# A ring of eleven places, unrolled programs and halved last loads in a mixer and MoE block

## The reference

```python
logits = xt @ w_router + b_router
top_val, top_idx = lax.top_k(logits, 4)          # of 32 experts
gate = softmax(top_val)
# for each expert e, on the tokens that chose it:
hdn = xb @ w_mlp1[e] + b_mlp1[e]                 # 1024 -> 2048
glu = minimum(hdn[:, :1024], 7); lin = clip(hdn[:, 1024:], -7, 7)
act = glu * sigmoid(1.702 * glu) * (lin + 1)
y = act @ w_mlp2[e] + b_mlp2[e]                  # 1024 -> 1024
# out = rmsnorm(x + sum_k gate_k * y_k) * norm_final_w
```

## Time and profile before

| | |
|---|---|
| median of 3 runs | 1125.36 us (1125.34 to 1125.79) |
| the profiled execution, its own time | 1125.41 us |
| its span | 1123.6 us |
| granted PE clock over the span | 0.998 |
| PE busy | 1085.1 us, 97% |
| DVE, ACT busy | 367.8 and 245.6 us |
| moved by DMA | 439.15 MB, mean 391 GB/s |
| the chain that ended last | PE 79%, DMA 14%, DVE 6% |

### The profile page before, as it was taken

One profiled execution on the slowest core, in us unless ns is written; L12 is line 12 of the kernel. 1 busy time (PEld: TensorE's weight loads), 2 busy tenths in 40 slices (PEclk: granted clock), 3 DMA queues, 4 the chain that ended last, 5 costly groups with the idle time before them and its releaser, 6 DMA issues.

```text
span 1123.6 us, 14458 instructions
## 1 busy us (share of the span) xinstructions
PE 1085.1 (97%) x5409; PEld 487.5 (43%) x5410; DVE 367.8 (33%) x813; ACT 245.6 (22%) x345; POOL 3.6 (0%) x12
## 2 busy tenths in 40 slices
PE   9999999999999999999999999999999999999996
PEld 8888888533333333333333333333333333333332
DVE  5977787422222222222222222222222222212223
ACT  4845674311111111111111111111111111111112
POOL 0000000000000000000000000000000000000000
PEclk9999999999999999999999999999999999999999
DMA  9655469999999999999999999999999999999996
GB/s 336 223 157 165 155 204 417 428 420 416 428 427 436 430 430 429 432 428 433 435 432 395 429 433 435 433 432 432 430 429 430 433 435 432 432 432 430 426 423 253
DMA packets 37877, 439.15 MB, mean 391 GB/s; under 512 B 5244, under 2 KB 5432, under 8 KB 21880
## 3 DMA queue, kind: packets, MB, share of 16 engines
q1 hardware_dynamic: 37488, 437.78, 93.3%
q10 hardware_dynamic: 360, 0.95, 0.3%
HBM read 437.67 MB, written 1.05 MB: 390 GB/s over the span
## 4 chain that ended last, share of the span: by engine, by line
PE 79%; DMA 14%; DVE 6%; issue 0%; ACT 0%; SPq 0%; DVEq 0%; PEldq 0%; ACTq 0%
PE bank L1154 33%; PE bank L1181 18%; DMA ring<-in_w_mlp_dram 11%; PE bank L798 9%; DMA late_slots<-in_w_mlp_dram 4%; PE bank L1083 3%; PE bank L1165 2%; PE bank L792 2%; PE bank L963 2%; PE bank L1011 2%; DVE xn L1670 2%; DVE xn L1667 2%; DVE xn L1674 2%; PE bank L1059 1%; PE bank L1067 1%; PE bank L1133 1%
## 5 line engine op out<-in xcount | busy, mean ns | idle before, releaser
L1154 PE MATMUL bank<-ring,xn 128*64 128x512 f32 x1232 | 276.3, 595 | 6.3 <-DMA ring<-in_w_mlp_dram 6.3
L1154 PE MATMUL bank<-late_slots,xn 128*64 128x512 f32 x880 | 197.5, 596 | 4.9 <-DMA late_slots<-in_w_mlp_dram 4.9
L1154 PEld LDWEIGHTS bank<-ring,xn 128*64 128x64 f32 x1232 | 84.4, 136 | 163.8 <-issue 150.3
L1181 PE MATMUL bank<-ring,smo 128*64 128x512 f32 x624 | 138.3, 595 | 0.0
L705 ACT ACTIVATE xn<-bank 128x512 f32<-128x512 f32 x33 | 19.7, 598 | 481.5 <-PE bank L1154 481.5
L1154 PEld LDWEIGHTS bank<-late_slots,xn 128*64 128x64 f32 x880 | 60.2, 136 | 117.9 <-issue 106.3
L1683 DVE SCALAR_TENSOR_TENSOR moe_y_lo<-bank,st,moe_y_hi 128x512 fp32r<-128x512 f32 x33 | 24.8, 750 | 235.5 <-ACT moe_y_hi L712 235.5
L1667 DVE TENSOR_SCALAR xn<-bank 128x512 f32<-128x512 f32 x33 | 22.8, 691 | 220.9 <-PE bank L1154 220.9
L1181 PE MATMUL bank<-late_slots,smo 128*64 128x512 f32 x416 | 92.1, 595 | 0.0
L1181 PEld LDWEIGHTS bank<-ring,smo 128*64 128x64 f32 x624 | 42.9, 137 | 81.1 <-issue 81.1
L712 ACT ACTIVATE moe_y_hi<-bank,st 128x512 fp32r<-128x512 f32 x33 | 22.7, 687 | 233.7 <-PE bank L1181 233.7
(11 more groups left out here) (270 smaller groups left out, 890.9 us busy)
## 6 DMA issues: line engine op xcount, KB each, us to landing
ring<-in_w_mlp_dram SPq DMA_DIRECT2D x43, 4096.0 KB, 30.4
late_slots<-in_w_mlp_dram SPq DMA_DIRECT2D x29, 4096.0 KB, 28.0
ring<-in_w_mlp_dram SPq DMA_DIRECT2D x28, 2048.0 KB, 13.4
late_slots<-in_w_mlp_dram SPq DMA_DIRECT2D x15, 2048.0 KB, 15.6
ring<-in_w_in_dram SPq DMA_DIRECT2D x22, 1024.0 KB, 5.4
late_slots<-in_w_mlp_dram SPq DMA_DIRECT2D x8, 1024.0 KB, 38.5
ring<-in_w_branch_dram SPq DMA_DIRECT2D x4, 1024.0 KB, 5.0
ring<-in_w_out_dram SPq DMA_DIRECT2D x4, 1024.0 KB, 7.1
```

The lines of the kernel that those rows point to most:

```text
L1154: last = mm(B[4 + u][g * C:(g + 1) * C, :], xgT[:, k % 4, k // 4, :], by_group(held[k // 2][0][:, k % 2, u * FF:(u + 1) * FF], g), start=F ...
L1181: last = mm(B[7][g * C:(g + 1) * C, :], actT[:, j, h * C:(h + 1) * C], held[4 + h][0][:, j // 2, (j % 2) * D + g * N:(j % 2) * D + (g + 1) ...
```

## The change

The place used once becomes the eleventh place of the ring: a chunk m sits in place m % 11 throughout. The places lie in two rows of memory, five in `late`, six in `ring`, and a quad of 4 MB must not cross the end of a row; so a pair whose first place is 3 or 9 is loaded as two DMAs of 2 MB. To give the eleventh place room beside `late`, `smo` is moved behind `sgm`. The order of the first 11 loads changes, their gates keep their counts. The loops of five experts are gone: SP's and PE's programs are written out for all experts (the run-time loop around each item stays). In the last loads of W1 (i = 3) and W2 (i = 5) the second MB is split into two halves of 0.5 MB, each with its own semaphore. The b2 scatter is issued before expert 16, not before expert 6. At the end, DVE takes the mean of the second tile between the two output halves of the first.

```diff
-PLACES = 10
-ROUND = PLACES // 2
-QUADS = range(ROUND + 1, E - 2)
+FIRST_QUADS = 6
+PLACES = 11
+QUADS = [m for m in range(CHUNKS * FIRST_QUADS, CHUNKS * (E - 2), 2) if m % PLACES not in (3, PLACES - 2)]
...
-        late_pair = [late[:, 2 * i:2 * i + 2, :] for i in range(4)]
-        places = [late_pair[1], pair[0], pair[1], pair[4], pair[5], pair[2], pair[3], late_pair[2], late_pair[3], late_pair[0]]
-        once = nc.alloc_sbuf_tensor_at("place_used_once", [P, 2, SLOT], F32, offset=sga_at)
+        late_pair = [late[:, 2 * i:2 * i + 2, :] for i in range(5)]
+        places = late_pair[1:5] + pair + late_pair[0:1]
+        quads = {n: late[:, at:at + 4, :] for n, at in ((PLACES - 1, 0), (0, 2), (1, 4), (2, 6))}
+        quads.update({4 + n: ring[:, 2 * n:2 * n + 4, :] for n in range(5)})
...
+        half_landed = {3: landed[4], 5: landed[5]}
...
                 if pieces == 2:
-                    for half, done in enumerate((place_landed[place], piece_landed[i])):
-                        sp.dma_start(places[place][:, half, :], src[:, half * SLOT:(half + 1) * SLOT]).then_inc(done, 16)
+                    at = [0, SLOT, 2 * SLOT] if i % 2 == 0 else [0, SLOT, SLOT + FF, 2 * SLOT]
+                    for a, b, done in zip(at, at[1:], (place_landed[place], piece_landed[i], half_landed.get(i))):
+                        sp.dma_start(places[place].rearrange("p a n -> p (a n)")[:, a:b], src[:, a:b]).then_inc(done, 16)
...
+            for e in range(E - 1):
+                after = sp.value_load(first_item[0:1, e + 1:e + 2], min_val=1, max_val=ITEMS - 1)
+                for i in range(CHUNKS):
+                    m = CHUNKS * e + i + PLACES
+                    if m >= CHUNKS * E:
+                        continue
+                    if m not in QUADS and m - 1 not in QUADS:
+                        wait_freed(after, i)
+                        load(m // CHUNKS, m % CHUNKS, m % PLACES, 2 if m >= CHUNKS * (E - 1) + 2 else 1)
+                    elif m - 1 in QUADS:
+                        wait_freed(after, i)
+                        load_quad(m // CHUNKS, m % CHUNKS // 2, (m - 1) % PLACES)
...
                     for u in range(2):
+                        if u and k == KB - 1 and 3 in in_halves:
+                            pe.wait_ge(*in_halves[3])
...
+                        if j == 3 and 4 + h in in_halves:
+                            pe.wait_ge(*in_halves[4 + h])
...
-            with pe.Fori(1, (E - 2) // ROUND) as r:
-                experts(r, lambda c: chunks_in_round(c, r))
+            for e in range(1, E - 1):
+                if e == E // 2:
+                    pe.wait_ge(opened, 2 * TT)
+                    scatter_b2()
+                first = after
+                after = pe.value_load(first_item[0:1, e + 1:e + 2], min_val=1, max_val=ITEMS - 1)
+                with pe.Fori(first, after) as i:
+                    item(i, chunks(e))
...
-            final_scale(0)
+            final_rstd(0)
+            final_half(0, 0)
             final_mean(1)
-            final_scale(1)
+            final_half(0, 1)
+            final_rstd(1)
+            final_half(1, 0)
+            final_half(1, 1)
```

More of the change, by code:

```diff
@@ L115, in landings @@
     for m in range(CHUNKS * E):
[L116 to L121, removed]
+        place = m % PLACES
+        if m - 1 in QUADS:
             table.append(table[-1])
@@ L158, in build @@
         xhi_at = late_at
-        late = nc.alloc_sbuf_tensor_at("late_slots", [P, 2 * HALF, SLOT], F32, offset=late_at)
+        late = nc.alloc_sbuf_tensor_at("late_slots", [P, 2 * HALF + 2, SLOT], F32, offset=late_at)
         xhi_room = sb("xhi_room", [P, KB, S])
@@ L406, in load_quad @@
                 sp.dma_start(quads[place].rearrange("p a n -> p (a n)"), src).then_inc(place_landed[place], 16)
+            def load_quad(e, g, place):
+                if g < 2:
+                    src = w_mlp1[0, e, g * N:(g + 1) * N, :].rearrange("(p s) n -> p (s n)", s=ROWS)
+                else:
+                    src = w_mlp2[0, e].rearrange("(p s) n -> p (s n)", s=2 * ROWS)
+                sp.dma_start(quads[place].rearrange("p a n -> p (a n)"), src).then_inc(place_landed[place], 16)
@@ L418, in _ @@
             sp.wait_ge(slots_used, Q_OUT + 2)
-            load(1, 0, 5)
-            load(1, 2, 7)
+            first_load(1)
+            first_load(6)
             sp.wait_ge(slots_used, Q_MOE)
-            load(1, 1, 6)
-            load(1, 3, 8)
-            load(1, 4, 9)
+            first_load(2)
+            first_load(7)
+            first_load(10)
             sp.wait_ge(firsts, 1)
[L427 to L442, removed]
+            for e in range(E - 1):
[5 more added lines that the diff above has]
+                    if m not in QUADS and m - 1 not in QUADS:
@@ L451, in _ @@
[L451 to L456, removed]
+                        load_quad(m // CHUNKS, m % CHUNKS // 2, (m - 1) % PLACES)
             after = sp.value_load(first_item[0:1, E - 1:E], min_val=1, max_val=ITEMS - 1)
-            wait_freed(after, 2)
+            wait_freed(after, 3)
@@ L1101, in chunks, with item @@
             def chunks(e):
[L1103 to L1122, removed]
+                at = [(m, *landing[m]) for m in range(CHUNKS * e, CHUNKS * (e + 1))]
+                return [(places[m % PLACES], place_landed[place], 16 * count) for m, place, count in at]
             def by_group(columns, g):
                 return columns.rearrange("p (q g s) -> p g q s", g=2, s=ROWS)[:, g]
-            def item(i, held, in_pieces={}):
+            def item(i, held, in_pieces={}, in_halves={}):
                 pe.wait_ge(row_ready, i + 1)
@@ L1184, in item @@
                     last.then_inc(slots_used, 2)
+            items = pe.value_load(first_item[0:1, E:E + 1], min_val=1, max_val=ITEMS - 1)
             with pe.Fori(0, after_first) as i:
[L1187 to L1202, removed]
-            with pe.Fori(1, (E - 2) // ROUND) as r:
-                experts(r, lambda c: chunks_in_round(c, r))
-            with pe.Fori(last_first, items) as i:
-                item(i, chunks(E - 1), {c: (piece_landed[c], 16 * (SLOTS[:Q_MOE].count(c - 2) + 1)) for c in piece_landed})
+                item(i, chunks(0))
+            after = after_first
+            for e in range(1, E - 1):
[6 more added lines that the diff above has]
+                    item(i, chunks(e))
+            with pe.Fori(after, items) as i:
+                item(i, chunks(E - 1), {c: (piece_landed[c], 16 * (SLOTS[:Q_MOE].count(c - 2) + 1)) for c in piece_landed},
+                     {3: (half_landed[3], 16 * (SLOTS[:Q_MOE].count(4) + 1)), 5: (half_landed[5], 16 * (SLOTS[:Q_MOE].count(5) + 1))})
             pe.wait_ge(gT_ready, items + 1)
@@ L1696, in final_scale, with final_half @@
                 dve.wait_ge(rstd, 2 * TT + t + 1)
[L1697 to L1700, removed]
+            def final_half(t, n):
+                cut = slice(n * N, (n + 1) * N)
+                v.scalar_tensor_tensor(out=xn[:, t, cut], in0=B[2 * t + n][:, :], scalar=st[:, 6 + t:7 + t],
+                                       in1=wfin[:, cut], op0=ALU.mult, op1=ALU.mult).then_inc(normed, 1)
             dve.wait_ge(s_small2, 16)
```

37 lines of the change are left out of this document (15 added, 22 removed).

## The result

| | before | changed | ratio, 95% interval |
|---|---|---|---|
| median of 7 runs | 1125.36 us | 1129.14 us | 1.0037 [1.0027, 1.0047] |
| profiled execution, its span | 1125.41, 1123.6 us | 1130.57, 1128.8 us | |

The change makes the kernel 3.8 us slower. 1127.2 was forecast, with 1122.6 to 1130.0 as the range: the time lies in the range, and the sign of the sum was right, but its size was half of what came. The profiled execution is one of the slower of the seven, 1.4 us above their median, so what its trace shows is somewhat larger than in the median run.

What follows compares the result with a forecast made beforehand. PE bounds roughly the first 25 experts, the weight stream the last ones. The terms sum to +1.8 us on the time before (median 1125.36), giving 1127.2 us, range 1122.6 to 1130.0.

Steps and rivals of the forecast that it cites:

- PE and SP written out: Weight stream after 503 us: some 22 more instruction blocks, three more visits to the worst DMA engine, +3.0 us.
- first dip, ring of eleven: Stream short of work at 240 to 260 us; eleven places let loads issue some 4 us sooner, -1.2 us.
- second dip: Stream dry at 590 to 610 us, the expert with two items; filling it gains 0, since late engines lose nothing there.
- 14 pairs: Weight loads: 14 of 72 quads become 28 loads of 2 MB at a slightly lower rate, +1.3 us.
- order of first loads: Expert 0's chunks 1 and 2 load later but still before PE reads them, 0 us.
- halves: PE's last W1 wait: four of eight records run before the last 0.5 MB lands, -1.0 us.
- mean: Final norm: DVE's earlier mean lets ScalarE's root overlap the second output half, -0.3 us.
- the blocks on single engines: Weight stream: each 16 KB instruction block delays one DMA engine by 1.1 us, and delays add up, +3.0 us.
- Ring and pairs: Weight stream: gain from eleven places, -1.2 and 0, against the cost of split quads, +1.3 us.
- (a): Weight stream: dips count in full, blocks shared evenly over engines; -2.1 us, 1123.3 us; chance 0.23 together with (c).
- (b): Weight stream: late engine hit more than three times more; beyond 1128.4 us, up to 1132; chance 0.27.
- (c): PE's loop end: unrolling removes a stall; 1127.2 us or up to 1 us better; 3 in 100, counted with (a).

Runs made afterwards that it cites:

- e1: Kernel before with only PE's program written out for experts 1 to 30, SP's loops and ten places kept; 1128.88 us, ratio 1.0026.
- e2: Kernel before with only SP's refills written out for all experts, PE's loop of five kept; 1125.61 us, ratio 1.0000.
- e8: Changed kernel with the old end: last MBs whole, second tile's mean after both output halves; 1129.90 us, ratio 1.0035.
- e9: Changed kernel with every load in 2 MB, no 4 MB quads left; 1131.82 us, ratio 1.0054.
- e4: Changed kernel with experts 24 to 29 loaded in 2 MB pairs instead of 4 MB quads; 1128.22 us, ratio 1.0019.
- e3: Kernel before with only the end edits: last MBs of W1 and W2 in halves, mean between output halves; 1124.51 us, ratio 0.9989.
- e5: Kernel before with SP written out and 16 extra unread loads of 16 KB, all on the same single DMA engine; 1137.82 us, ratio 1.0114.

## Why the prediction came out as it did

| step | predicted | measured | by |
|---|---|---|---|
| PE and SP written out | +3.0 | +3.3 (1.9 to 3.9), all of it PE's | e1, e2 |
| first dip, ring of eleven | -1.2 | both dips -1.6, an estimate; with the pairs -0.4 | traces of e8 and e1 |
| second dip | 0 | in the same -1.6 | traces of e8 and e1 |
| 14 pairs | +1.3 | +1.15 | e9 against e4 |
| order of first loads | 0 | no wait in item 0 in the trace | trace |
| halves | -1.0 | -0.8 in the kernel before, 0 in the changed one | e3, trace |
| mean | -0.3 | -0.5 | both traces |
| drop of PE's clock | not in the sum | +2.1 in the median, +2.95 in the profiled run | e4 and e9, trace |

**Right.** The step that decided the sign, the blocks on single engines, was right in mechanism and within 10% in size. The count of 22 blocks after 500 was exact. "They go round a part of the engines" is now a number: the plateau at half rate shows eight. 22 / 8 = 2.75 visits at 1.1 us are 3.0, near the landings 3.2 to 3.3 us later in e1. That the end moved by 3.3 as well is in part chance, since the last landing came 4.70 later and the wait of 1.20 went. Ring and pairs were put at +0.1 and came at -0.4 in the landings, within the bounds of their terms.

**Wrong in size.** The sum was 2.0 us short, and two terms make that up. The first is missing: the prediction let PE's waits grow ("13 to 15 us") without asking what a longer single wait does. In fact they summed to 11.8, in fewer and longer pieces, and behind the longest the clock went down, +2.1 us in the median. The length of the wait alone does not tell when: the changed kernel's 2.39 at 1014.63, e8's 2.20 and e1's 2.12 were followed by matmuls at full speed, while a shorter one in e5 was not (3.65 would be full speed):

```profile
926.13 5.28 PE L1152 MATMUL bank<-late_slots,xn 128*64 128x512 f32 x16 [2.09 <-DMA late_slots<-in_w_mlp_dram]
```

The second is the halves, -1.0 forecast and 0 measured in the changed kernel. Together these are 3.1 us; the other terms came out 0.4 us better in sum by the table, and some 0.7 us stays unaccounted for between traces and medians. That the time still lies in the range is in part luck: the upper end was there for blocks that add up faster, which they did not, and the clock used that room.

**Halves.** They pay only where the last wait is at the last k. In the changed kernel, as in e1, PE came late out of the wait at 1045 and found everything after it landed, so the predicted -1.0 became 0 (e8 against the changed kernel: 0.8 in all with the mean's 0.5, not told from 0.5 by these runs). The prediction named this condition (a wait over 0.97) but took the old wait for granted.

**Rivals.** (a) is refuted by e1 and e5. (b) is where the median lies, between its 1128.4 and 1132; e1 shows that the blocks alone gave 3.3, not 4.2, so (b)'s price was reached by other causes on top, the clock and the halves. (c): there was no stall at the loop's end to gain.

What is not settled: how the dips' 1.6 us divide between the first and the second, since neither was filled alone, and what decides whether the clock drops after a wait of 2.1 to 2.4 us.

## What to carry to other kernels

In a kernel whose end is set by a stream of loads, look at the slope with which the stream dies away, in windows of 1 us: a plateau at half or at one sixteenth of the rate shows that engines are late, and then the mean GB/s does not tell the time. Anything small that runs on few DMA engines, instruction blocks above all, is to be priced at its time on the engine it hits, so code that streams weights should loop in a body that its engine can keep. And where PE must wait, several short waits are better than one long one: 16 waits of at most 1.6 us left the clock up (e4), one of 3.62 cost 2.95 us more.

## What the hardware showed that was not expected

- Instruction blocks fall on eight of the sixteen DMA engines: share 0.48 to 0.52 for four microseconds at the changed kernel's end, 0.49 and 0.50 in e1, and packet durations that repeat every eight blocks.
- A small DMA costs all engines about 0.2 us beside its bytes: 16 loads of 16 KB over all engines, 3.3 us. Splitting a load of 4 MB into two of 2 MB costs 0.08 us.
- After PE waits of 3.62, 2.50 and (in e8) 2.39 and 2.29 us, and in e5 of 2.09, the granted clock was 0.50 for some 3 to 7 us while PE was busy; after waits of 2.39 us in the changed kernel and 2.20 in e8 it was not.
- Two dips of 1.2 and 2.4 us by the mean rates were worth some 1.6 us of landing time (an estimate from e8, e1, e4 and e9).
